# A four-layer transformer on one core: layer 0's x, turned on TensorE or loaded already turned

## The reference, cut to what matters

```python
h = rmsnorm(x, gain) @ w_in          # w_in: 2048 x 6160 to 9224, f32
q, k, v, gates, ... = split(h)       # attention or recurrence of several kinds, layer by layer
y = concat(ya, yb)                   # 256 x 2048
x = x + y @ w_out                    # w_out: 2048 x 2048
```

## Time and profile before

| | us |
|---|---|
| median of 3 runs (lowest, highest) | 1983.82 (1981.48, 1984.71) |
| profiled execution, its own time | 1984.74 |
| its span | 1982.9 |
| PE busy in the span | 1946.5 (98%) |
| DVE busy | 1165.8 (59%) |
| ACT busy | 1007.1 (51%) |
| POOL busy | 180.0 (9%) |
| mean granted clock of TensorE | 0.991 |

### The profile page before, as it was taken

How to read it: one execution, slowest core, us unless ns; L and a number is a source line. 1 busy time by engine, 2 the same in 40 slices (tenths; PEclk the granted TensorE clock), 3 DMA queues, 4 the chain that set the end, 5 groups by cost and what they waited for, 6 DMA issues and landing times.

```text
span 1982.9 us, 29116 instructions
## 1 busy us (share of the span) xinstructions
PE 1946.5 (98%) x12032; PEld 1750.4 (88%) x12032; DVE 1165.8 (59%) x1621; ACT 1007.1 (51%) x1543; POOL 180.0 (9%) x164
## 2 busy tenths in 40 slices
PE   8999999999999999989999999999999999999997
PEld 8988888888899989889899899888889989988886
DVE  5445554454556676778566556655556656654554
ACT  5345445654556545755553344456454344445643
POOL 0000010110003121301001001000000100100110
PEclk9999999999999999999999999999999999999999
DMA  7555555555554344444555654555555555455453
GB/s 265 170 191 170 170 191 176 159 166 180 187 163 139 128 139 139 148 129 157 183 180 191 194 171 146 167 183 165 175 186 183 178 191 168 152 191 170 164 198 128
DMA packets 172852, 338.52 MB, mean 171 GB/s; under 512 B 9536, under 2 KB 9920, under 8 KB 172592
## 3 DMA queue, kind: packets, MB, share of 16 engines
q1 hardware_dynamic: 171632, 332.89, 51.2%
q0 software_dynamic: 944, 3.61, 0.7%
q10 hardware_dynamic: 144, 0.16, 0.0%
HBM read 334.54 MB, written 2.10 MB: 170 GB/s over the span
## 4 chain that ended last, share of the span: by engine, by line
PE 94%; DVE 3%; ACT 1%; issue 1%; DMA 0%; SPq 0%; DVEq 0%; ACTq 0%
PE ACC L657 17%; PE ACC L655 17%; PE ACC L656 17%; PE ACC L662 11%; PE ACC L663 11%; PE ACC L664 11%; DVE WL L1266 1%; DVE S L1487 1%; PE PM L762 1%; PE PM L678 1%; PE PM L750 1%; PE PM L784 1%; PE PM L785 1%; PE PM L783 1%; ACT WH L958 1%
## 5 line engine op out<-in xcount | busy, mean ns | idle before, releaser
L1266 DVE TENSOR_TENSOR WL<-RAW,WH 128x1024 fp32r<-128x1024 f32 x624 | 788.5, 1277 | 630.2 <-ACT WH L958 628.6
L958 ACT ACTIVATE WH<-RAW 128x1024 fp32r<-128x1024 f32 x626 | 654.7, 1055 | 569.1 <-PE ACC L657 310.2
L662 PE MATMUL ACC<-XH,WH 128*128 128x256 f32 x1920 | 554.1, 289 | 4.6 <-DVE WL L1266 4.5
L663 PE MATMUL ACC<-XL,WH 128*128 128x256 f32 x1920 | 545.9, 284 | 0.0
L664 PE MATMUL ACC<-XH,WL 128*128 128x256 f32 x1920 | 545.6, 284 | 0.0
L655 PE MATMUL ACC<-WH,XH 128*128 128x512 f32 x1024 | 406.4, 397 | 0.0
L657 PE MATMUL ACC<-WH,XL 128*128 128x512 f32 x1024 | 399.0, 390 | 0.0
L656 PE MATMUL ACC<-WL,XH 128*128 128x512 f32 x1024 | 398.6, 389 | 0.0
L662 PEld LDWEIGHTS ACC<-XH,WH 128*128 128x128 f32 x1920 | 371.3, 193 | 7.0 <-DVE WL L1266 5.6
L663 PEld LDWEIGHTS ACC<-XL,WH 128*128 128x128 f32 x1920 | 371.2, 193 | 0.9
L664 PEld LDWEIGHTS ACC<-XH,WL 128*128 128x128 f32 x1920 | 371.0, 193 | 0.0
(11 more groups left out here) (327 smaller groups left out, 1704.9 us busy)
## 6 DMA issues: line engine op xcount, KB each, us to landing
RAW<-in_ev_w_in SPq DMA_DIRECT2D x71, 1024.0 KB, 4.9
RAW<-in_w_in_ab SPq DMA_DIRECT2D x64, 1024.0 KB, 5.5
RAW<-in_w_in_c SPq DMA_DIRECT2D x64, 1024.0 KB, 5.4
RAW<-in_od_w_in SPq DMA_DIRECT2D x48, 1024.0 KB, 5.1
RAW<-in_ev_w_out SPq DMA_DIRECT2D x16, 1024.0 KB, 4.9
RAW<-in_od_w_out SPq DMA_DIRECT2D x16, 1024.0 KB, 4.9
RAW<-in_w_out_ab SPq DMA_DIRECT2D x16, 1024.0 KB, 4.9
RAW<-in_w_out_c SPq DMA_DIRECT2D x16, 1024.0 KB, 4.9
```

What stands on the lines that cost most here:

```text
L662: e.matmul(o, wh, xh, start=f and g % 2 == 0, stop=False, skip_group_check=True)
L663: e.matmul(o, wh, xl, start=False, stop=False, skip_group_check=True)
L958: e.activation(hi, src, ACT.Copy).then_inc(s_hi)
L1266: e.tensor_tensor(lo, src, hi.bitcast(F32), ALU.subtract).then_inc(s_lo)
```

## The change

Four things are changed.

1. The host also hands over x turned, `xT`, laid out as [128, 16 x 256] with k tile n in columns 256n to 256n+255: 2048 KB more to load. It is loaded in five parts of 2, 2, 4, 4 and 4 k tiles (256, 256, 512, 512 and 512 KB) into Y, which is free at that time. A step `x0`, for q = 0 to 7, takes the place of `xt` in layer 0: ACT and DVE read Y in place of PSUM, and PE does nothing.
2. SP's loads stand in another order, with W1 and W2 ahead of most of x. The constants, `ident` among them, come in one piece behind everything else. X is still loaded, for the squares and the residual.
3. `squares` and `rms_a` have later slots.
4. A step `warm` ahead of everything: DVE zeroes a piece of S5, ACT copies one column of it (its table load comes with that), and PE multiplies zeros, 4 products of 128x512. POOL issues its bias blocks only when the row factors are spread.

```diff
+WARM = 4
+        X_PARTS = ((0, 2), (2, 2), (4, 4), (8, 4), (12, 4))
+
         def begin_plan():
+            put(-1, "warm")
             for q in range(8):
-                put((-1, -0.5, 0.5, 2.5)[q // 2], "xt", q, 1)
+                put((-1, -0.5, 0, 1, 2, 3, 4, 5)[q], "x0", q)
             for b in range(4):
-                put((-0.5, 0.5, 2.5, 4)[b], "squares", b)
-            put(5, "rms_a", 0)
+                put((3, 3.5, 4.5, 5)[b], "squares", b)
+            put(5.5, "rms_a", 0)
             put(6.5, "rms_b", 0, 1)
...
-            e.dma_start(C[:, 0:n_id], I["const"][:, 0:n_id]).then_inc(s_c0, 16)
-            load_x(0)
+            def load_xT(i):
+                c = slice(256 * X_PARTS[i][0], 256 * sum(X_PARTS[i]))
+                e.dma_start(Y[:, c], I["xT"][:, c]).then_inc(s_xT[i], 16)
+
+            load_xT(0)
             first = RAW[0][:, :].rearrange("p (k n) -> p k n", k=4)
             e.dma_start(first[:, 0:2, :], weights(0)[:, 0:2, :]).then_inc(s_first, 16)
             e.dma_start(first[:, 2:4, :], weights(0)[:, 2:4, :]).then_inc(s_raw[0], 16)
+            load_xT(1)
+            load(1)
+            load_xT(2)
+            load(2)
+            load_x(0)
             load_x(1)
-            load(1)
+            load_xT(3)
             load_x(2)
             load_x(3)
-            e.dma_start(C[:, n_id:n_dil], I["const"][:, n_id:n_dil]).then_inc(s_c1, 16)
-            e.dma_start(RB[:, :], I["row"].partition_broadcast(128)).then_inc(s_c1, 16)
-            load(2)
+            load_xT(4)
+            e.dma_start(C[:, 0:n_dil], I["const"][:, 0:n_dil]).then_inc(s_con, 16)
+            e.dma_start(RB[:, :], I["row"].partition_broadcast(128)).then_inc(s_con, 16)
...
+            def warm(_, b):        # on PE
+                e.wait_ge(s_warm, 1)
+                for _ in range(WARM):
+                    e.matmul(PM[0][:, :], S5[:, 1024:1152], S5[:, 1024:1536], start=True, stop=True)
...
+            def warm(_, b):        # on ACT
+                e.wait_ge(s_warm, 1)
+                e.activation(unused, S5[:, 1024:1025], ACT.Copy)
+
+            def x0(q, _):
+                if q == 0:
+                    e.wait_ge(s_vec, 16)
+                for i, (k, n) in enumerate(X_PARTS):
+                    if k == 2 * q:
+                        e.wait_ge(s_xT[i], 16)
+                for n in (2 * q, 2 * q + 1):
+                    e.activation(XH3[:, n, :], Y[:, 256 * n:256 * n + 256], ACT.Copy, scale=gains[0][:, n:n + 1]).then_inc(s_xh)
...
+            def warm(_, b):        # on DVE
+                e.memset(S5[:, 1024:1536], 0.0).then_inc(s_warm)
+
+            def x0(q, _):
+                e.wait_ge(s_xh, 2 * q + 2)
+                for n in (2 * q, 2 * q + 1):
+                    e.scalar_tensor_tensor(XL3[:, n, :], Y[:, 256 * n:256 * n + 256], gains[0][:, n:n + 1],
+                                           XH3[:, n, :].bitcast(F32), ALU.mult, ALU.subtract).then_inc(s_xl)
...
                 e.reciprocal(rstd, rstd).then_inc(s_rstd)
+                if layer == 0:
+                    e.wait_ge(s_con, 32)
...
             def norm_qk(_, b):     # on POOL
+                e.wait_ge(s_row, 1)
                 load_bias(0)
                 load_bias(1)
```

More of the change, by code:

```diff
@@ L494, in around @@
             return ([x for s in (p - 0.5,) for x in plan.get(s, ())], plan.get(p, ()))
-        s_c0, s_c1, s_mask, s_lam, s_tab, s_gw, s_fin, s_first, s_out = (
-            sem(n) for n in ("s_c0", "s_c1", "s_mask", "s_lam", "s_tab", "s_gw", "s_fin", "s_first", "s_out"))
+        s_vec, s_con, s_warm, s_mask, s_lam, s_tab, s_gw, s_fin, s_first, s_out = (
+            sem(n) for n in ("s_vec", "s_con", "s_warm", "s_mask", "s_lam", "s_tab", "s_gw", "s_fin", "s_first", "s_out"))
         s_x = [sem(f"s_x{i}") for i in range(4)]
+        s_xT = [sem(f"s_xT{i}") for i in range(len(X_PARTS))]
         s_raw = [sem(f"s_raw{i}") for i in range(NRAW)]
@@ L560, in program @@
         x_rows = I["x"].rearrange("(t p) c -> p t c", p=128)
-        n_id, n_cos, n_dil = COFF["flip"][0], COFF["cos"][0], COFF["dilated"][0]
+        n_cos, n_dil = COFF["cos"][0], COFF["dilated"][0]
         block = ctx.enter_context(nc.Block())
@@ L665, in products @@
                 m.then_inc(s_mm)
+            def warm(_, b):
+                e.wait_ge(s_warm, 1)
+                for _ in range(WARM):
+                    e.matmul(PM[0][:, :], S5[:, 1024:1152], S5[:, 1024:1536], start=True, stop=True)
             def xt(i, b):
                 layer, q = divmod(i, 8)
[L669 to L674, removed]
+                e.wait_ge(s_evD, at_D(layer - 1, "out", q // 2))
                 o = bank(b)
@@ L683, in rms_b @@
             def rms_b(layer, b):
-                if layer == 0:
-                    e.wait_ge(s_c1, 32)
                 e.wait_ge(s_diag, layer + 1)
@@ L928, in gate_lru @@
                 read_out[b] = (s_li, 2 * n + 2)
-            steps = {"xt": xt, "rms_b": rms_b, "gates1": gates1, "gates2": gates2, "decay": decay, "mscores": mscores, "qkT": qkT,
+            steps = {"warm": warm, "xt": xt, "rms_b": rms_b, "gates1": gates1, "gates2": gates2, "decay": decay, "mscores": mscores, "qkT": qkT,
                      "scores": scores, "pT": pT, "pv": pv, "ty": ty, "decays1": decays1, "decays3": decays3, "norm_sum": norm_sum,
@@ L950, in scalar @@
         def scalar(e):
-            e.dma_start(VC[:, :], I["vec"]).then_inc(s_c0, 16)
+            e.dma_start(VC[:, :], I["vec"]).then_inc(s_vec, 16)
             def split(p):
@@ L1016, in evacuate @@
                                      accum_out=ssq[:, 4 * t + J.b:4 * t + J.b + 1]).then_inc(s_sq)
+            def warm(_, b):
[9 more added lines that the diff above has]
+                    e.activation(XH3[:, n, :], Y[:, 256 * n:256 * n + 256], ACT.Copy, scale=gains[0][:, n:n + 1]).then_inc(s_xh)
             def xt(i, b):
                 layer, q = divmod(i, 8)
-                if i == 0:
-                    e.wait_ge(s_c0, 32)
-                e.wait_ge(s_xt, i + 1)
+                e.wait_ge(s_xt, i - 7)
                 for kk in range(2):
@@ L1231, in subln @@
                     e.activation(ss, ss, ACT.Sqrt, bias=vec("eps"), scale=1.0 / 256).then_inc(s_sln)
-            steps = {"xt": xt, "squares": squares, "root": root, "rms_a": rms_a, "gates1": gates1, "decay": decay, "pT": pT,
+            steps = {"warm": warm, "x0": x0, "xt": xt, "squares": squares, "root": root, "rms_a": rms_a, "gates1": gates1, "decay": decay, "pT": pT,
                      "norm_qk": norm_qk, "qkT": qkT, "scores": scores, "pv": pv, "ty": ty, "conv": conv, "decays1": decays1,
@@ L1695, in subln @@
                         e.scalar_tensor_tensor(y, y, ss[:, t, h:h + 1], row("subln"), ALU.mult, ALU.mult).then_inc(s_sub)
-            steps = {"xt": xt, "rms_a": rms_a, "rms_b": rms_b, "gates1": gates1, "gates2": gates2, "decay_row": decay_row,
+            steps = {"warm": warm, "x0": x0, "xt": xt, "rms_a": rms_a, "rms_b": rms_b, "gates1": gates1, "gates2": gates2, "decay_row": decay_row,
                      "decay": decay, "mscores": mscores, "norm_qk": norm_qk, "scale_qk": scale_qk, "scores": scores, "pT": pT, "pv": pv,
@@ L1889, in arrange @@
     m["x"] = _np.ascontiguousarray(a["x"][0])
+    m["xT"] = _np.ascontiguousarray(a["x"][0].T.reshape(16, 128, 256).transpose(1, 0, 2).reshape(128, 4096))
     t, c = _np.arange(128)[:, None], _np.arange(32)[None, :]
```

## The result

Four runs of the changed kernel gave 1992.33, 1991.91, 1992.54 and 1995.45 us, median 1992.43; the kernel before had 1983.92 beside them. The ratio on record is 1.005, 95% interval 1.0036 to 1.0064 (the two medians alone give 1.0043): 8.5 us slower by the medians, clear of noise. The range of 1985.5 to 1996 holds it, and the forecast of 1991.7 is 0.7 us off. The span of the profiled execution is 1990.5 us.

A forecast was written before the change was run, and what follows sets the result against it. PE, busy for 98% of the span, was taken to bound the kernel. P7 6.4 us late plus 1.5 for the clock gave 1984.74 + 7.9 = 1992.6 profiled, 1991.7 as median; range 1985.5 to 1996 (8 in 10).

The forecast's parts named there:

- The front: PE's start: P0 near 9.0 and not 12.68, fewer turns, a higher clock; together 6.2 us gained.
- The turns: PE, between the first pieces: two groups of turns fall away, about 1.4 us gained.
- the half pace: PE's first 12 products: 0.12 us each and not 0.21 if zeros keep the clock up, 1.1 us gained.
- W3's landing: SP's load queue: 1792 KB more ahead of W3, so it lands at 28.4 (27.2 to 28.9), not 24.3.
- P5's wait: PE ahead of P5: the 6.2 us gained turn into a wait of about 7 us, until 31.1.
- The row behind W3: ACT's splits, squares and XH after W3 lands: 11.56 us; P7 starts 14.3 us after landing, 6.4 us late.
- The clock: PE at P7 and P8 after idle waits: a lower clock costs between nothing and 3.3 us, taken as 1.5.
- (a): Load queue: W3 passes the loads ahead of it, P7 starts about 5 us early, 1978.5 us; chance 0.08.
- (b): Load queue: faster than 400 GB/s, clock holds, W3 at 26, P7 4.0 us late, 1987 us; chance 0.15.
- (c): PE's clock falls in both waits, stays low through P7, P8 and more: 10 to 12 us, 1995; chance 0.17.
- (d): PE's start: zeros do not raise the clock, time as forecast; chance counted within the forecast's 0.60.
- The sum: At P7 and so at the end: 6.4 + 1.5 = 7.9 us later.

The follow-up runs named there:

- experiment 5: The kernel before with x loaded once more (2048 KB) into the free Y just ahead of W3: 1989.23 us, ratio 1.0026.
- experiment 6: The kernel before with POOL's two bias blocks issued only when the row factors are spread: 1981.99 us, ratio 0.9991.
- experiment 11: The kernel before with late bias blocks and the first constants loaded 512 columns wide, not 128: one execution, 1982.5 us.
- Experiment 3: The changed kernel with W3 loaded ahead of x, and XH, squares and row factors written ahead of W4's split: 1978.45 us, ratio 0.9974.
- Experiment 1: The changed kernel, loads untouched, with layer 0's XH, XL, squares and row factors written ahead of W3's first split: 1982.85 us, ratio 0.9995.
- experiment 2: The changed kernel, written order untouched, with W3 loaded ahead of x and of xT's last part: 1989.58 us, ratio 1.0031.
- experiment 7: The changed kernel with PE multiplying zeros in its waits, 8 products ahead of P5 and 4 ahead of the row factors: 1990.23 us, ratio 1.0031.
- the closer version: Experiment 3 with k tiles 4 and 5 ahead of W1, fewer constants ahead of W4, early Sqrt table, row factors' product behind P7: 1975.79 us, ratio 0.9955.

## Why the prediction was right, step by step

- **The front.** P0 at 8.11 against 9.0 forecast: W0's first half landed at 5.7 (issued at 1.19, 4.5 us), not at 6.6. The 6.6 does not follow from its own rows either: 5.6 and 192 to 256 KB more at 400 GB/s make 6.1 to 6.3. The turns came to 1.35 us and the half pace to 1.2, as forecast, but the latter was read from one trace, and experiments 5, 6 and 11 show that the time at half pace differs from one kernel to the next (1.2, 2.1 and 4.0 us from P0's start). In all the front gave about 7.1 us and not 6.2, and lost 1.1 again in the wait ahead of P2. Experiment 3 shows 5.3 of it at the mark once the loads and the order no longer bury it.
- **W3's landing.** 28.3 against 28.4, inside 27.2 to 28.9. Of the 1.7 us by which a faster start could help I took less than a third, without working it out. The trace gives half: 245 and 390 GB/s from 2 to 6 us are 1270 KB and not 936, 0.8 us at 400 GB/s, which makes 28.1. So the bytes added, over the rate, give the landing, and how much of the slow start would go was a guess.
- **P5's wait.** 7.07 us until 31.18, against "about 7" and 31.1. The end of the wait was worked out; its length agrees by luck. PE "free near 24" was to be 30.2 less 6.2 plus 1, and that is 25.0, which would make a wait of 6.1. PE was free at 24.1 because the front gave 0.9 us more. Neither figure enters the sum. Experiment 1 shows that the wait comes from the order on ACT: with the XH ahead of the split there is no wait.
- **The row behind W3.** Its terms added up to 11.56 and it took 11.8 (28.33 to 40.11); the mark came 14.3 us after the landing, against 14.0. This was the larger term, and experiments 2 and 5 show both its halves: it hurts behind W4 just as behind W3, and with the old, shorter row the mark comes 4.7 us sooner after W3's landing. Two of its signs were off: ACT idled for 8.81 us ahead of W3 and not 7 to 8, and PE for 3.27 us ahead of the row factors and not 4 to 5, as P5 ran 22 products at half pace (to 36.02).
- **The clock.** 1.5 us forecast, 1.5 measured by experiment 7. That was luck in part: it was a middle between two ends and not a derivation, and the upper end was off too (7 us at 0.21 for 0.12 lose 3.0 us, not 3.3). Experiment 1 shows the weakness: there the same question had the other answer (2.2 us), and my expectation left it out. By the rule of the Trainium skill's page TensorE: Matmul & The Clock Gate (Part 1: The HAM clock gate), that an idle PE falls back to 1.2 GHz, the clock falls in such a wait, and the traces agree: the stretch from 31 to 38 us has 0.63. Its price is set by how much of the slow stretch falls on products that nothing hides.
- **Rivals.** (a), W3 passing the others, did not happen: in the changed kernel, as before, no load of SP's queue landed ahead of one issued before it. (b), a faster queue, did not either: 402 GB/s from 6 to 25 us, and W3 at 28.3 and not 26. Of (c) half is true: the clock fell in both waits, but it was back within P7. (d), that the zeros make no difference here, holds, though for the reason given (PE has time to spare) and not because they don't raise the clock: P0 ran at 0.12.
- **The sum.** 6.4 + 1.5 = 7.9 forecast; 6.63 + 1.55 = 8.18 at the split behind P7.

## What to carry to other kernels

When the start is bound by memory, what a load costs is not its own time but what lands later behind it in the queue: work out the landing of the first load that a later piece needs, for the order before and after, in bytes over the rate that the trace shows. Then look at each engine's written row: whatever stands behind an instruction that waits for that load waits too, though its own data may have been there for long: the XH of k tiles 10 and 11 was made at 29.3 from a load that had landed by 18.6. And judge a gain at the front at the point where the next wait ends; here 6 us turned into idle time at P5. Moving the steps alone brought the kernel level with before, and moving W3 ahead of x as well gave 5.3 us of them at the mark.

## What the runs showed of the hardware

- The rate of the first microseconds goes with the first load. With 64 KB in rows of 512 bytes first, the stretch from 4 to 6 us moved 169 to 204 GB/s (the kernel before, experiments 5 and 6); with 256 KB in rows of 2 KB first, 361 to 390. From 2 to 4 us it is the other way round, 276 to 306 against 202 to 265. Whether the length of the rows or the bytes do it is not shown.
- A load of SP's landed sooner without two small blocks that POOL issues at the start: PE could take the second quarter of x at 11.06 and 11.13 with them (the kernel before, experiment 5) and at 10.12 and 10.34 without (experiments 6 and 11).
- PE's pace is at half after 2.99 us without work in experiment 1, and stays there for the 24 products of P6. Zeros keep it up: PE was granted 1.00 from 25 to 50 us with them in the waits (experiment 7), where the changed kernel has 0.77 to 40 us and 0.83 behind.
- The clock column says 1.00 for the first 15 us of the kernel before, where products are 0.21 apart; at the start of an execution the pace of the products is to be read, not this column.
- One table load is enough for Copy, Square and Sqrt, if Sqrt's comes first: ACT of the closer version has no second one in its first 50 us, while the kernels that start with Copy's load again ahead of Sqrt (at 40.11 in the changed kernel).
